# A four-layer decoder trunk: the first gather in three parts, the last down unit in column halves, TensorE's branch before the last quad

## The chip, the cores and the metric

The kernel runs on one core of one Trainium2 chip. The metric is the device time of one execution in microseconds (us), the median of several runs. Everything is float32.

## The reference

The input x is 256 tokens of 1024 values. Four layers each apply a token mixer (layer 0 and 3 forgetting attention, 1 HGRN2, 2 a short convolution), then a mixture of experts; each is followed by a LayerNorm of a scaled residual:

```
for layer in range(DEPTH):
    x = layer_norm(DEEPNORM_ALPHA * x + mixed, ln_mix_g[layer], ln_mix_b[layer])
    ffn = hierarchical_moe(x, ...)
    x = layer_norm(DEEPNORM_ALPHA * x + ffn, ln_ffn_g[layer], ln_ffn_b[layer])

# in hierarchical_moe: top-1 of 4 groups, then top-2 of its 8 experts; gates is zero for all other experts
hg = jnp.einsum('btd,edf->btef', x, w_gate)
hu = jnp.einsum('btd,edf->btef', x, w_up)
h = jax.nn.silu(hg) * hu * gates[..., None].astype(x.dtype)
return jnp.einsum('btef,efd->btd', h, w_down)
```

There are 32 experts a layer, each with a hidden width of 256, so a layer's expert weights are 100 MB and have to be read once whatever the tokens choose.

## The kernel before

**Weights.** All large weights are packed by the host into units of 2 MB (128 partitions x 4096 floats). SyncE loads them in the order of use, on one queue, into 11 slots: 6 of `ring` and, while the expert stage lasts, 5 in `work`. A unit that needs a slot waits for `unit_used`, the semaphore that TensorE raises when it has finished with the unit that was there (line 494 issues the loads).

**The expert stage.** The 32 experts are taken in 8 quads of 4. Each expert gets a window of 32 token places, so a quad fills TensorE's 128 columns as four tiles of 32. A quad has six units: 0 to 3 hold gate and up weights, 4 and 5 the down weights of output columns 0 to 511 and 512 to 1023. For a quad TensorE does, in this order: a gather (a product of x with a 0/1 selection matrix `sel`, eight blocks of 128 features; line 930), which ScalarE copies out of PSUM with the norm's scale and bias as `xw` (line 1088); units 0 to 3, each two feature blocks (line 954); transposes of the hidden values (964, 967); unit 4 and unit 5 (`down`, line 984), after each of which VectorE (h = 0) or ScalarE (h = 1) copies the sums to `y_sb`; and after each copy `combine` (line 992), which scatters the result back into the token rows in PSUM banks 4 to 7. The next quad's gather lies between these steps. Only the first quad's gather has nothing ahead of it: TensorE makes all eight blocks, four into bank 1 and four into bank 2, and then starts with unit 0.

**The last quad.** It has three `keep_busy` pairs of idle matmuls (line 651) between its gate units. Its last unit arrives as two DMAs of 1 MB, one for each half of the hidden width (j = 0 and 1), and `down(1)` waits for `half_in` in the middle. The order is down(0), down(1), combine(0), combine(1). `half_ready` follows combine(0), `z_ready` each token block of combine(1).

**The norm.** VectorE takes statistics of the first 512 columns when `half_ready` is there (line 1375), of the second 512 at `z_ready` (1352), then ScalarE and VectorE make the inverse root and x; TensorE transposes x (657) and starts the next mixer.

**The branch.** A window of 32 places may be too small for an expert. Then a second path (`experts_more`, behind `more_path`) runs. With these inputs it is never taken: every engine reads the flag `most`, and jumps over that code (lines 472 and 473). TensorE does it behind the last quad.

**ScalarE's tables.** The Silu of the quads needs another table than the norm's logarithm and exponential; line 1296 loads the latter behind the branch.

Of the kernel before, what the change touches and what calls it, by code (L numbers as in the profile page):

```python
# [263 lines left out]
def build(nc, a, out):  # L264
    with ExitStack() as ctx:
# [132 lines left out]
        unit_used, half_ready = sem("unit_used"), sem("half_ready")  # L398
        bank_filled = sem("bank_filled")
# [236 lines left out]
        def _(pe):  # L636
# [284 lines left out]
            def gather(sems, n, par, half, to=1):  # L921


                pe.wait_ge(sems["sel_made"], n + 1)
                if to == 1:
                    pe.wait_ge(sems["xw_ready"], n * 2 + (half + FREE))
                for i in range(4):
                    for c in range(TC):
                        xk = x[:, c, (4 * half + i) * P:(4 * half + i + 1) * P]
                        last = nc.tensor.matmul(psum[:, to, i * P:(i + 1) * P], xk, sel[:, par, c, :],  # L930
                                                start=(c == 0), stop=(c == TC - 1))
                last.then_inc(sems["gathered"], 1)

            def quad(sems, n, par, slots, ahead, last_quad):
# [4 lines left out]
                for u in range(GU):  # L939
# [4 lines left out]
                    if u % (GU // 2) == 0:  # L944

                        pe.wait_ge(sems["xw_ready"], n * 2 + (u // (GU // 2) + 1 + FREE))
# [27 lines left out]
                def down(h):  # L974

                    pe.wait_ge(*slots[GU + h][1])
                    w = slots[GU + h][0].rearrange("p (j e c) -> p e j c", e=QE, j=FC)
                    for j in range(FC):
                        if j and h == NH - 1 and last_quad and sems is first:

                            pe.wait_ge(half_in, 16 * (n // NQ + 1))
                        for e in range(QE):
                            rows = slice(W * e, W * (e + 1))
                            last = nc.tensor.matmul(psum[rows, 2 + h, :], hT[:, j, rows], w[:, e, j],  # L984
                                                    start=(j == 0), stop=(j == FC - 1))
                    last.then_inc(sems["unit_used"], 1)

                def combine(h):

                    pe.wait_ge(sems[("y0_ready", "y1_ready")[h]], n + (1 + FREE))  # L990
                    for c in range(TC):
                        last = nc.tensor.matmul(psum[:, 4 + NH * c + h, :], hT[:, FC + c, :], y_sb[:, h * HB:(h + 1) * HB],  # L992
                                                start=False, stop=last_quad, skip_group_check=True)
                        if last_quad and sems is first and h == NH - 1:
                            last.then_inc(z_ready, 1)
                    if last_quad and sems is first and h == 0:
                        last.then_inc(half_ready, 1)
# [14 lines left out]
            def experts(l):  # L1012
                gather(first, l * NQ, 0, 0)
                gather(first, l * NQ, 0, 1, 2)
                for q in range(NQ):
                    units = [("moe", l, q * QU + u) for u in range(QU)]
                    quad(first, l * NQ + q, q % 2, [(slot(*u), landed(*u)) for u in units], q < NQ - 1, q == NQ - 1)
# [12 lines left out]
            for l in range(DEPTH):  # L1030
# [32 lines left out]
                experts(l)  # L1063
                runs = more_path(pe, l, runs, experts_more)
# [8 lines left out]
        def _(act):  # L1073
# [163 lines left out]
            def tokens(l, sems, n, par, half, at=1):  # L1237

                act.wait_ge(sems["gathered"], n * 2 + half + 1)
                for i in range(4):  # L1240
                    ins = scaled(2 * l, 4 * half + i, xw[:, 4 * half + i, :], psum[:, at, i * P:(i + 1) * P])
                ins.then_inc(sems["xw_ready"], 1)

            def quad(l, sems, n, par, ahead):
# [507 lines left out]
```

## Time and profile before

| | us |
|---|---|
| median of 3 runs | 1525.01 (1524.22 to 1525.95) |
| the profiled execution, its own time | 1522.0 |
| its span, first to last instruction | 1520.1 |
| TensorE busy | 1348.7 (89%) |
| VectorE / ScalarE busy | 336.7 / 314.3 |
| weights read | 478.36 MB, 315 GB/s over the span |

The profile gives busy times by engine and by line, the chain of work that ended last, and for any stretch the clock granted to TensorE (1.00 is 2.4 GHz, 0.50 is 1.2 GHz) and what the DMA engines moved. A matmul in float32 appears as two weight loads and two matmul records; so 8 matmuls of a down unit are 16 records.

### The profile page before, as it was taken

Reading aid. Unit: us, or ns where it says so; the run is one execution under the profiler, and the core shown is the slowest. Engines: PE = TensorE matmul, PEld = TensorE weight load, DVE = VectorE, ACT = ScalarE, POOL = GpSimd, SP = SyncE. Lnnn points to the kernel's source line nnn. Section 1 sums busy time; section 2 is a strip of 40 time slices with the busy share of each in tenths; the row PEclk is TensorE's granted clock in tenths of the full one; section 3 lists DMA queues with packets and bytes.
Section 4 is the critical chain, followed back from the end, with each engine's and each line's share of the span. In section 5 each row is a group of like instructions: output and inputs, shape, how many; then the busy total and the mean of one; then the engine's idle time right before and its main releaser. Section 6 shows DMA issues by size and latency. Waiting matters only on the chain.

```text
span 1520.1 us, 18503 instructions
## 1 busy us (share of the span) xinstructions
PE 1348.7 (89%) x7798; PEld 763.6 (50%) x7798; DVE 336.7 (22%) x879; ACT 314.3 (21%) x766; POOL 64.2 (4%) x99
## 2 busy tenths in 40 slices
PE   8999988778999979988789999888789999988775
PEld 7766633323664765433226875333328775533321
DVE  0243311002101972211002033101011252301102
ACT  0242312112112321222112002221111252321110
POOL 2200000000000520000000000000001100000000
PEclk9999999999999989999999999999999999999998
DMA  9756499999644008799999844999998355599995
GB/s 326 282 207 237 178 430 427 427 427 425 256 166 164 3 23 365 300 427 426 429 426 424 336 169 172 410 427 427 428 426 345 136 222 221 216 429 427 427 426 233
DMA packets 35766, 480.74 MB, mean 316 GB/s; under 512 B 4304, under 2 KB 4624, under 8 KB 6368
## 3 DMA queue, kind: packets, MB, share of 16 engines
q1 hardware_dynamic: 34416, 476.92, 75.9%
q0 software_dynamic: 1120, 2.09, 0.8%
q8 instruction: 67, 1.10, 0.3%
q10 hardware_dynamic: 144, 0.48, 0.1%
q14 instruction: 19, 0.16, 0.0%
HBM read 478.36 MB, written 1.05 MB: 315 GB/s over the span
## 4 chain that ended last, share of the span: by engine, by line
PE 65%; DMA 23%; DVE 7%; ACT 3%; issue 2%; SPq 1%; DVEq 0%
DMA ring<-in_units 17%; PE psum L692 15%; PE psum L954 9%; PE psum L706 9%; PE psum L727 7%; PE psum L930 6%; DMA work<-in_units 5%; PE psum L984 5%; PE psum L992 5%; ACT work L1088 2%; DVE work L1499 1%; PE psum L714 1%; PE psum L657 1%; PE psum L1046 1%; PE psum L767 1%
## 5 line engine op out<-in xcount | busy, mean ns | idle before, releaser
L692 PE MATMUL psum<-xT,ring 128*128 128x256 f32 x1024 | 222.4, 379 | 1.0 <-DMA ring<-in_units 0.5
L692 PEld LDWEIGHTS psum<-xT,ring 128*128 128x128 f32 x1024 | 194.2, 190 | 28.3 <-issue 1.4
L992 PE MATMUL psum<-work 128*128 128x512 f32 x256 | 126.7, 620 | 42.9 <-DVE work L1651 22.8
L954 PE MATMUL psum<-ring,work 128*32 128x512 f32 x1200 | 143.3, 611 | 23.4 <-DMA ring<-in_units 23.4
L930 PE MATMUL psum<-work,x 128*128 128x128 f32 x1024 | 131.3, 283 | 35.3 <-ACT work L1088 35.0
L930 PEld LDWEIGHTS psum<-work,x 128*128 128x128 f32 x1024 | 120.8, 194 | 71.6 <-issue 68.2
L706 PE MATMUL psum<-ring,xT 128*128 128x512 f32 x320 | 138.6, 593 | 0.4 <-ACT xT L1088 0.4
L1088 ACT ACTIVATE work<-psum,affine_t 128x128 f32<-128x128 f32 x256 | 96.4, 457 | 123.8 <-PE psum L930 123.8
L1646 DVE TENSOR_TENSOR work<-work,psum 128x256 f32<-128x256 f32 x32 | 13.5, 421 | 485.5 <-ACT work L1247 485.5
L954 PE MATMUL psum<-work 128*32 128x512 f32 x848 | 104.2, 627 | 14.5 <-DMA work<-in_units 14.5
L727 PE MATMUL psum<-ring,work 128*128 128x512 f32 x256 | 112.0, 593 | 0.5 <-DVE work L1562 0.5
L992 PEld LDWEIGHTS psum<-work 128*128 128x128 f32 x256 | 44.0, 190 | 130.9 <-DVE work L1651 48.2
L1084 ACT ACTIVATE work<-psum 128x512 f32<-128x512 f32 (+2 forms) x116 | 61.1, 541 | 230.2 <-PE psum L706 131.0
L706 PEld LDWEIGHTS psum<-ring,xT 128*128 128x128 f32 x320 | 60.5, 190 | 74.8 <-issue 74.5
L954 PEld LDWEIGHTS psum<-ring,work 128*32 128x32 f32 x1200 | 36.3, 110 | 119.4 <-issue 96.1
L1247 ACT ACTIVATE work<-psum 128x256 f32<-128x256 f32 x32 | 12.3, 384 | 338.6 <-PE psum L954 338.6
L727 PEld LDWEIGHTS psum<-ring,work 128*128 128x128 f32 x256 | 47.7, 190 | 56.2 <-issue 55.5
L984 PE MATMUL psum<-ring,work 128*32 128x512 f32 x528 | 66.1, 617 | 9.9 <-DMA ring<-in_units 9.9
L954 PEld LDWEIGHTS psum<-work 128*32 128x32 f32 x848 | 26.2, 113 | 86.5 <-issue 72.4
L984 PE MATMUL psum<-work 128*32 128x512 f32 x496 | 59.8, 598 | 3.0 <-DMA work<-in_units 3.0
L1253 ACT ACTIVATE work<-psum 128x512 f32<-128x512 f32 x32 | 19.1, 597 | 176.8 <-PE psum L984 176.8
L1651 DVE COPY work<-psum 128x512 f32<-128x512 f32 x32 | 22.1, 692 | 137.0 <-PE psum L984 137.0
(197 smaller groups left out, 1104.7 us busy)
## 6 DMA issues: line engine op xcount, KB each, us to landing
ring<-in_units SPq DMA_DIRECT2D x138, 2048.0 KB, 27.2
work<-in_units SPq DMA_DIRECT2D x83, 2048.0 KB, 26.3
ring<-in_units SPq DMA_DIRECT2D x6, 1024.0 KB, 45.8
ring<-in_units SPq DMA_DIRECT2D x4, 512.0 KB, 8.4
work<-in_units SPq DMA_DIRECT2D x2, 1024.0 KB, 44.9
x<-in_x SPq DMA_DIRECT2D x2, 512.0 KB, 4.6
out<-x SPq DMA_DIRECT2D x2, 512.0 KB, 3.1
work<-in_tables SPq DMA_DIRECT2D x1, 768.0 KB, 30.9
```

Source lines behind the costliest of these rows:

```text
L657: last = nc.tensor.transpose(bank(key, P, i * P), t, ident)
L692: last = nc.tensor.matmul(bank(key, T, s * T), w[:, 2 * m + s, k, :], xT[:, k, :], start=(k == 0), stop=(k == KD - 1))
L706: last = nc.tensor.matmul(bank(key), xT[:, k, c * P:(c + 1) * P], w[:, k, :], start=(k == 0), stop=(k == KD - 1))
L727: last = nc.tensor.matmul(psum[:, 4 + NH * c + h, :], lhs[:, k, c * P:(c + 1) * P], w[:, k, :], start=False, stop=(k == KD - 1), skip_grou ...
L930: last = nc.tensor.matmul(psum[:, to, i * P:(i + 1) * P], xk, sel[:, par, c, :], start=(c == 0), stop=(c == TC - 1))
L954: last = nc.tensor.matmul(psum[rows, 0, :].rearrange("p (t f) -> p t f", t=2), xw[:, k, rows], w[:, e, kk], start=(k == 0), stop=(k == KD ...
L984: last = nc.tensor.matmul(psum[rows, 2 + h, :], hT[:, j, rows], w[:, e, j], start=(j == 0), stop=(j == FC - 1))
L992: last = nc.tensor.matmul(psum[:, 4 + NH * c + h, :], hT[:, FC + c, :], y_sb[:, h * HB:(h + 1) * HB], start=False, stop=last_quad, skip_gr ...
L1084: nc.scalar.activation(dst, src, func, **kw).then_inc(drained_by["A"], 1)
L1088: return nc.scalar.activation(dst, src, ACT.Identity, scale=affine_t[:, j, 0, k:k + 1], bias=affine_t[:, j, 1, k:k + 1])
L1253: nc.scalar.activation(y_sb[:, HB:D], psum[:, 3, :], ACT.Copy).then_inc(sems["y1_ready"], 1)
L1651: v.tensor_copy(y_sb[:, 0:HB], psum[:, 2, :]).then_inc(sems["y0_ready"], 1)
```

## The change

1. **First gather.** For a layer's first quad, TensorE gathers blocks 0 and 1 (bank 1), then 2 and 3 (bank 2), runs unit 0, and gathers blocks 4 to 7 behind it (`gather_blocks` and `token_blocks` are the old loops, over the blocks that they are given). ScalarE copies the first pair out and raises `pair_ready`, for which unit 0 waits.
2. **Last down unit.** The host packs the second down unit of every quad in two column halves (256 output columns each) instead of two halves of the hidden width. In a layer's last quad the halves are used one after the other: a product of 256 columns into a bank of its own, ScalarE's copy of 256 columns, a combine of 256 columns, and the same again for the second half, which waits for `half_in`. combine(0) and with it `half_ready` now stand between down(0) and the first half.
3. **The branch.** TensorE reads `most` and branches before the last quad. The last quad's code stands in both arms; in the arm that runs, nothing follows it.
4. **ScalarE's table.** The norm's table is loaded behind the last quad's Silu.

TensorE's program, around a layer's first gather. L930 and L954 are the gather and the gate units before, L926 and L966 the same after; the waits are semaphores. Before:

```order
L930 MATMUL psum<-work,x 128x128 [waits drained_dve,sel_made_1,drained_act,xw_ready_1]
L930 MATMUL psum<-work,x 128x128 x7
L930 MATMUL psum<-work,x 128x128 [waits sel_made_1]
L930 MATMUL psum<-work,x 128x128 x7
L954 MATMUL psum<-ring,work 32x512 [waits unit_in2,xw_ready_1,h_ready_1]
L954 MATMUL psum<-ring,work 32x512 x7
L954 MATMUL psum<-ring,work 32x512 [waits unit_in3]
L954 MATMUL psum<-ring,work 32x512 x7
```

and in the changed kernel:

```order
L926 MATMUL psum<-work,x 128x128 [waits drained_dve,drained_act,sel_made_1]
L926 MATMUL psum<-work,x 128x128 x7
L966 MATMUL psum<-ring,work 32x512 [waits unit_in2,pair_ready,h_ready_1]
L966 MATMUL psum<-ring,work 32x512 x7
L926 MATMUL psum<-work,x 128x128 [waits xw_ready_1,sel_made_1]
L926 MATMUL psum<-work,x 128x128 x7
L966 MATMUL psum<-ring,work 32x512 [waits unit_in3,xw_ready_1]
L966 MATMUL psum<-ring,work 32x512 x7
```

Half of the gather has moved from ahead of the first gate unit to behind it, and that unit waits for a pair of blocks only.

TensorE's program at a layer's end, from the last quad's down(0) on. L984 and L992 are down and combine before, L999 and L1028 the same after, L1010 and L1019 those in halves. Before:

```order
L984 MATMUL psum<-ring,work 32x512 [waits unit_in4,y0_ready_1,hT_ready_1]
L984 MATMUL psum<-ring,work 32x512 x7
L984 MATMUL psum<-ring,work 32x512 [waits unit_in5]
L984 MATMUL psum<-ring,work 32x512 x3
L984 MATMUL psum<-ring,work 32x512 [waits half_in]
L984 MATMUL psum<-ring,work 32x512 x3
L992 MATMUL psum<-work 128x512 [waits y0_ready_1]
L992 MATMUL psum<-work 128x512
L992 MATMUL psum<-work 128x512 [waits y1_ready_1]
L992 MATMUL psum<-work 128x512
L472 TENSOR_LOAD most [waits most_ready]
```

and in the changed kernel:

```order
L999 MATMUL psum<-ring,work 32x512 [waits unit_in4,y0_ready_1,hT_ready_1]
L999 MATMUL psum<-ring,work 32x512 x7
L1028 MATMUL psum<-work 128x512 [waits y0_ready_1]
L1028 MATMUL psum<-work 128x512
L1010 MATMUL psum<-ring,work 32x256 [waits unit_in5]
L1010 MATMUL psum<-ring,work 32x256 x7
L1019 MATMUL psum<-work 128x256 [waits third_ready]
L1019 MATMUL psum<-work 128x256
L1010 MATMUL psum<-ring,work 32x256 [waits half_in]
L1010 MATMUL psum<-ring,work 32x256 x7
L1019 MATMUL psum<-work 128x256 [waits y1_ready_1]
L1019 MATMUL psum<-work 128x256
```

combine(0) has moved ahead of the last unit, each of whose halves is now followed by a wait for ScalarE and a combine; the branch has left this place.

TensorE's program in the changed kernel at the new place of the branch, ahead of the last quad:

```order
L1028 MATMUL psum<-work 128x512 [waits y1_ready_1]
L1028 MATMUL psum<-work 128x512
L1098 TENSOR_LOAD most [waits most_ready]
L1098 ISA x2
L1099 COMPARE_AND_BRANCH
L966 MATMUL psum<-ring,work 32x512 [waits unit_in0,xw_ready_1,h_ready_1]
```

The reading of the flag now stands between the last combine of quad 6 and quad 7's unit 0. In program order the arm for the overflow comes first: a whole quad (72 matmuls) and then `experts_more` (72 more); the arm that runs stands behind both. Before, the jump went over `experts_more` alone.

The diff, cut to its core:

```diff
+            def first_gather(n):
+                pe.wait_ge(first["sel_made"], n + 1)
+                gather_blocks(0, (0, 1), 1).then_inc(pair_gathered, 1)
+                gather_blocks(0, (2, 3), 2, 2).then_inc(first["gathered"], 1)
...
+                    if first_quad and u == 0:
+                        pe.wait_ge(pair_ready, n // NQ + 1)
+                    elif u % (GU // 2) == 0 or first_quad and u == 1:
                         pe.wait_ge(sems["xw_ready"], n * 2 + (u // (GU // 2) + 1 + FREE))
...
                     last.then_inc(sems["unit_used"], 1)
+                    if first_quad and u == 0:
+                        gather(sems, n, par, 1)
...
+                def last_down(b):
+                    pe.wait_ge(*((half_in, 16 * (n // NQ + 1)) if b else slots[GU + 1][1]))
+                    w = slots[GU + 1][0].rearrange("p (b j e c) -> p b e j c", b=2, e=QE, j=FC)
+                    for j in range(FC):
+                        for e in range(QE):
+                            rows = slice(W * e, W * (e + 1))
+                            last = nc.tensor.matmul(psum[rows, (3, 0)[b], 0:HB // 2], hT[:, j, rows], w[:, b, e, j],
+                                                    start=(j == 0), stop=(j == FC - 1))
+                    last.then_inc(unit_used if b else third_filled, 1)
+                def last_combine(b):
+                    pe.wait_ge(*((first["y1_ready"], n + (1 + FREE)) if b else (third_ready, n // NQ + 1)))
+                    cols = slice(b * HB // 2, (b + 1) * HB // 2)
+                    for c in range(TC):
+                        last = nc.tensor.matmul(psum[:, 4 + NH * c + 1, cols], hT[:, FC + c, :], y_sb[:, HB:D][:, cols],
+                                                start=False, stop=True, skip_group_check=True)
+                        if b:
+                            last.then_inc(z_ready, 1)
...
-                if last_quad:
+                if last_quad and sems is first:
                     down(0)
-                    down(1)
-                    combine(0)
-                    last = combine(1)
+                    combine(0).then_inc(half_ready, 1)
+                    for b in range(2):
+                        last_down(b)
+                        last_combine(b)
...
-                experts(l)
-                runs = more_path(pe, l, runs, experts_more)
+                experts(l, range(NQ - 1))
+                pe.wait_ge(most_ready, l + 1)
+                over = pe.value_load(most[0:1, l:l + 1], min_val=0, max_val=1)
+                with pe.If(over > 0):
+                    experts(l, [NQ - 1])
+                    experts_more(l, runs)
+                with pe.Else():
+                    experts(l, [NQ - 1])
+                runs = over + runs
...
+            def first_tokens(l):
+                act.wait_ge(pair_gathered, l + 1)
+                token_blocks(l, 0, (0, 1), 1).then_inc(pair_ready, 1)
+                act.wait_ge(first["gathered"], l * NQ * 2 + 1)
+                token_blocks(l, 0, (2, 3), 2).then_inc(first["xw_ready"], 1)
...
                 nc.scalar.activation(silu_g, psum[:, 0, 0:ED], ACT.Silu).then_inc(sems["silu_ready"], 1)
+                if last_quad:
+                    nc.scalar.preload_act_table_set("natural_log_exp_and_others")
...
+                    act.wait_ge(third_filled, l + 1)
+                    nc.scalar.activation(y_sb[:, HB:HB + HB // 2], psum[:, 3, 0:HB // 2], ACT.Copy).then_inc(third_ready, 1)
                 act.wait_ge(sems["unit_used"], n * QU + (QU + spare(sems)))
-                nc.scalar.activation(y_sb[:, HB:D], psum[:, 3, :], ACT.Copy).then_inc(sems["y1_ready"], 1)
+                if last_quad:
+                    nc.scalar.activation(y_sb[:, HB + HB // 2:D], psum[:, 0, 0:HB // 2], ACT.Copy).then_inc(sems["y1_ready"], 1)
...
+        down = inputs["moe_w_down"][l].reshape(NQ, QE, FC, P, NH, 2, HB // 2)
+        moe[:, GU] = down[:, :, :, :, 0].transpose(0, 3, 2, 1, 4, 5).reshape(NQ, P, UNIT)
+        moe[:, GU + 1] = down[:, :, :, :, 1].transpose(0, 3, 4, 2, 1, 5).reshape(NQ, P, UNIT)
```

## Rows read from the trace of the kernel before

**Rows 1.** The page: span, and TensorE instruction queue: packets, MB, share.

```profile
span 1520.1 us, 18503 instructions
q8 instruction: 67, 1.10, 0.3%
```

**Rows 2.** Windows: us, busy (records) by engine, PEclk, DMA share, GB/s.

```profile
168.00:178.00 10.00, 9.05 (x65) 5.71 (x67) 5.05 (x25) 3.74 (x10) 0.00 (x0) 1.00 0.06 15
180.00:290.00 110.00, 95.10 (x696) 41.00 (x688) 12.81 (x25) 22.53 (x52) 0.00 (x0) 1.00 1.00 427
290.00:363.00 73.00, 55.53 (x352) 20.68 (x352) 6.17 (x11) 8.37 (x21) 0.00 (x0) 0.95 1.01 427
1305.00:1314.00 9.00, 8.04 (x64) 5.45 (x66) 4.40 (x22) 3.40 (x10) 0.00 (x0) 1.00 0.00 0
```

**Rows 3.** Timeline, PE then ACT, the first gather of layer 0: start us, us.

```profile
172.11 3.81 PE L930 MATMUL psum<-work,x 128*128 128x128 f32 x32
175.85 7.07 PE L954 MATMUL psum<-ring,work 128*32 128x512 f32 x64
174.17 1.51 ACT L1088 ACTIVATE work<-psum,affine_t 128x128 f32<-128x128 f32 x4 [3.71 <-PE psum L930]
175.96 1.51 ACT L1088 ACTIVATE work<-psum,affine_t 128x128 f32<-128x128 f32 x4 [0.28 <-PE psum L930]
```

**Rows 4.** Timeline, SyncE: issues of weight units after that gather.

```profile
177.84 5.48 SPq L494 DMA_DIRECT2D ring<-in_units  x4
190.53 9.54 SPq L494 DMA_DIRECT2D work<-in_units  x3
```

**Rows 5.** Timeline, PE: one combine of quad 0, and the down unit behind it.

```profile
191.29 1.98 PE L992 MATMUL psum<-work 128*128 128x512 f32 x4 [0.81 <-DVE work L1651]
193.20 1.92 PE L984 MATMUL psum<-work 128*32 128x512 f32 x16
```

**Rows 6.** Timeline, PE, the end of layer 0's mixture of experts.

```profile
358.68 1.92 PE L984 MATMUL psum<-ring,work 128*32 128x512 f32 x16 [1.47 <-DMA ring<-in_units]
361.07 1.07 PE L984 MATMUL psum<-ring,work 128*32 128x512 f32 x8 [0.47 <-DMA ring<-in_units]
363.55 1.07 PE L984 MATMUL psum<-ring,work 128*32 128x512 f32 x8 [1.41 <-DMA ring<-in_units]
364.55 3.70 PE L992 MATMUL psum<-work 128*128 128x512 f32 x8
```

**Rows 7.** Timeline, DVE then ACT, the same end.

```profile
360.66 0.69 DVE L1651 COPY work<-psum 128x512 f32<-128x512 f32 x1 [2.73 <-PE psum L984]
366.64 1.30 DVE L1375 BATCH_NORM_STATS2 small<-psum 128x6 f32<-128x512 f32 x2 [5.29 <-PE psum L992]
367.85 0.68 DVE L1352 BATCH_NORM_STATS2 small<-psum 128x6 f32<-128x512 f32 x1
355.66 0.38 ACT L1247 ACTIVATE work<-psum 128x256 f32<-128x256 f32 x1 [16.57 <-PE psum L954]
```

**Rows 8.** Timeline, PE, layer 1's HGRN scores: small matmuls in a row.

```profile
512.35 0.55 PE L876 MATMUL psum<-work 128*64 128x64 f32 x14
```

**Rows 9.** Windows with the clock down, the ends of layers 1 and 3.

```profile
803.70:807.10 3.40, 3.40 (x10) 0.95 (x11) 0.00 (x0) 1.40 (x2) 0.00 (x0) 0.50 0.99 417
1496.60:1500.00 3.40, 2.79 (x16) 0.90 (x20) 0.00 (x0) 0.00 (x0) 0.00 (x0) 0.51 0.97 405
```

**Rows 10.** Timeline, PE, layer 1's last quad: unit 3, half of 5.

```profile
793.77 1.92 PE L954 MATMUL psum<-ring,work 128*32 128x512 f32 x16 [0.97 <-DMA ring<-in_units]
803.64 1.90 PE L984 MATMUL psum<-ring,work 128*32 128x512 f32 x8 [1.41 <-DMA ring<-in_units]
```

**Rows 11.** Lines 472 and 473, TensorE's flag and jump: ns min/median/max, by line.

```profile
L472 PEldq TENSOR_LOAD <-most x4: 297/318/494, 365.3 to 1504.9; - x4
L473 PEldq COMPARE_BRANCH  x4: 313/350/428, 366.2 to 1505.5; - x4
```

**Rows 12.** DMA packets from 3.2 to 4.6 us behind layer 0's branch.

```profile
q8 instruction: 1, 0.02, 5.5%
```

More of the change, by code:

```diff
@@ L919, in convolution, with gather_blocks, gather, quad @@
                 output_projection(l, yT)
-            def gather(sems, n, par, half, to=1):
-                pe.wait_ge(sems["sel_made"], n + 1)
[L925 to L934, printed above, removed]
+            def gather_blocks(par, blocks, to, at=0):
+                for i, k in enumerate(blocks):
+                    for c in range(TC):
+                        last = nc.tensor.matmul(psum[:, to, (at + i) * P:(at + i + 1) * P], x[:, c, k * P:(k + 1) * P], sel[:, par, c, :],
+                                                start=(c == 0), stop=(c == TC - 1))
+                return last
+            def gather(sems, n, par, half):
+                pe.wait_ge(sems["sel_made"], n + 1)
+                pe.wait_ge(sems["xw_ready"], n * 2 + (half + FREE))
+                gather_blocks(par, range(4 * half, 4 * half + 4), 1).then_inc(sems["gathered"], 1)
+            def first_gather(n):
+                pe.wait_ge(first["sel_made"], n + 1)
+                gather_blocks(0, (0, 1), 1).then_inc(pair_gathered, 1)
+                gather_blocks(0, (2, 3), 2, 2).then_inc(first["gathered"], 1)
+            def quad(sems, n, par, slots, ahead, last_quad, first_quad=False):
                 pe.wait_ge(sems["h_ready"], n + FREE)
@@ L976, in down @@
                     pe.wait_ge(*slots[GU + h][1])
[L977 removed]
+                    if h:
+                        w = slots[GU + h][0].rearrange("p (b j e c) -> p e j b c", b=2, e=QE, j=FC)
+                    else:
+                        w = slots[GU + h][0].rearrange("p (j e c) -> p e j c", e=QE, j=FC)
                     for j in range(FC):
[L979 to L981 removed]
                         for e in range(QE):
                             rows = slice(W * e, W * (e + 1))
[L984 removed]
+                            to = psum[rows, 2 + h, :]
+                            last = nc.tensor.matmul(to.rearrange("p (b c) -> p b c", b=2) if h else to, hT[:, j, rows], w[:, e, j],
                                                     start=(j == 0), stop=(j == FC - 1))
                     last.then_inc(sems["unit_used"], 1)
+                def last_down(b):
[10 more added lines that the diff above has]
+                    cols = slice(b * HB // 2, (b + 1) * HB // 2)
+                    for c in range(TC):
+                        last = nc.tensor.matmul(psum[:, 4 + NH * c + 1, cols], hT[:, FC + c, :], y_sb[:, HB:D][:, cols],
+                                                start=False, stop=True, skip_group_check=True)
+                        if b:
+                            last.then_inc(z_ready, 1)
                 def combine(h):
@@ L1010, in quad, with experts @@
                     last.then_inc(more["combined"], 1)
[L1012 to L1015, printed above, removed]
+            def experts(l, quads):
+                if 0 in quads:
+                    first_gather(l * NQ)
+                for q in quads:
                     units = [("moe", l, q * QU + u) for u in range(QU)]
-                    quad(first, l * NQ + q, q % 2, [(slot(*u), landed(*u)) for u in units], q < NQ - 1, q == NQ - 1)
+                    quad(first, l * NQ + q, q % 2, [(slot(*u), landed(*u)) for u in units], q < NQ - 1, q == NQ - 1, q == 0)
             def experts_more(l, runs):
@@ L1261, in experts @@
                 for par in range(2):
-                    quad(l, first, l * NQ + NQ - 2 + par, par, par == 0)
+                    quad(l, first, l * NQ + NQ - 2 + par, par, par == 0, par == 1)
             def experts_more(l, runs):
@@ L1270, in experts_more @@
                         quad(l, more, n, 0, False)
+                nc.scalar.preload_act_table_set("natural_log_exp_and_others")
             act.wait_ge(affine_in, 16)
```

28 lines of the change are left out of this document (14 added, 14 removed).

## The prediction

> **What bounds the kernel now.** I read the page first, then the clock and the DMA by windows, then the two seams of a layer in the timeline. TensorE is busy 89% of the span, but that average hides two kinds of stage. In the mixers the engine is the bound. In the expert stage it is so only at the beginning, where 11 slots are already full. From the first freed slot on, the queue of weights runs at 427 GB/s without a pause to the end of the stage, whatever TensorE does [rows 2]: 37 of the 48 units of 2.10 MB at 427 GB/s are 182 us, and layer 0's loads, first issued at 177.84 [rows 4], end with the last half at 363.5 [rows 6]. So three things set a layer's expert stage: when the first slot comes free, the bandwidth, and what stands between the last landing and the norm. Between the last prefetch and the first freed slot the queue idles (15 GB/s in layer 0, nothing in layer 3) [rows 2]. The chain of waits books much of this under TensorE lines; the flat 427 GB/s says that the stage's length is the queue's.
>
> **First gather.** Before, the gather of 32 records starts at 172.11 and unit 0 at 175.85 [rows 3]. ScalarE starts on the first half at 174.17, that is 2.06 after the gather's start. With 8 records in the first part instead of 16, and 3.81/32 = 0.12 for a record, it starts 0.95 earlier, at 173.22; two copies of four that take 1.51 are 0.8, so the pair is ready at 174.0. TensorE has made the second pair by then too (16 records, 1.9). Allow 0.1 for the signal: unit 0 starts at about 174.15, **1.7 us earlier**, and the first load is issued at 176.1 instead of 177.84 [rows 3, 4]. It is alone in the queue for 4.9 us. The next slot comes free behind the second half of the gather (1.9) and unit 1, at about 180.0 by the same lag, before the first load has ended (181.0 at the earliest), so the queue never runs dry, and all later loads are 1.7 earlier. TensorE gains nothing itself: the 3.7 us of gather are still there, partly behind unit 0, so unit 3 ends 0.2 to 0.4 later than before. That is harmless, since TensorE later waits for weights anyway (55.5 busy of 73 us in the second part of the stage) [rows 2]; the third gate unit needs blocks 4 and 5, whose copy (1.51) lies beside unit 1 (1.75). Four layers: **-6.8 us**. Bounds: -7.6, if the pair were ready as soon as its gather ends, and -4.8, if each of the two signals costs 0.25 more.
>
> **The end of the stage.** Here the reordering has a price that is easy to overlook. Before, down(0) starts at 358.68 when its unit lands, the halves of the last unit wait for their landings (361.07, 363.55), and VectorE's statistics of the second 512 columns start at 367.85, held by the combine(0) that comes last and by two statistics of 0.65 each [rows 6, 7]. That is 9.17 behind down(0)'s start. After the change TensorE's own chain is longer than the landings: y0's copy starts 1.98 behind down(0) and takes 0.69, and 0.05 later combine(0) starts: 2.7 [rows 6, 7]. combine(0) holds TensorE 1.91 (193.20 - 191.29) [rows 5]: 4.65. A half down unit has 16 records of 256 columns; I take half the column time of a whole one, 0.85, and the same 0.27 to the copy's start: 5.8. ScalarE copies 256 columns in 0.38 [rows 7], plus 0.05: 6.2. The combine of 256 columns is 0.85 + 0.2: 7.25. The second half landed at 4.9, so it starts at once: 1.1, copy 0.43, first token block 0.43 + 0.3: 9.5, and VectorE starts at **9.55 instead of 9.17**. So the end gains nothing and loses 0.4 a layer: the work moved out from behind the last landing is put in front of it, where only 0.5 + 1.4 us were free [rows 6], and two round trips to ScalarE are added. Upper bound: if a half unit took a whole one's 1.92, as its number of records is the same, it would be 2 x 0.87 more, 2.1 a layer. The nearest row speaks against it: 14 matmuls of 64 columns and fewer pass in 0.55 us, 0.04 each [rows 8], where a record of 256 columns needs 0.053. Lower bound: statistics at the second half's landing (4.9) plus 1.1, 0.43 and 0.8, that is 7.2 and -1.9 a layer, reached only if nothing of the chain ahead counted.
>
> **The clock.** In layer 1 the clock was at 0.50 (1.2 GHz) for 3.4 us right on the last half and combine(0), behind a stretch in which TensorE mostly waited; the half took 1.90 instead of 1.07. In layer 3 such a dip lay from 1496.6 to 1500.0, on its down(0) [rows 6, 9, 10]. Layer 1's dip cost 1.6 at its place. The new order puts down(0) and combine(0) on the chain too, so a dip on any of 9.5 us counts instead of 5, while TensorE idles less there. I take one more layer's 0.6 off for layer 1 and nothing for layer 3: end of stage in all **+1.0** (from -2.5 to +3.5).
>
> **ScalarE's table** costs nothing at either place: 1.3 us before, it lay between the last copy and the first root, and now beside TensorE's wait for unit 4. If it stayed behind the branch it would now be late, by about 0.5.
>
> **The branch.** TensorE's reading of the flag takes 0.3 to 0.5 us and its jump 0.35 [rows 11]; with the steps between them I put it at 1.3. At the new place it hides beside quad 6's last combine (four records, 1.91) [rows 5], since the sequencer runs ahead of the array. Behind it are three `keep_busy` pairs and units; unit 3 still waits 0.97 for its landing and down(0) another 0.6 to 0.7 behind the hidden values' copy (of the 1.47 shown, part is the copy) [rows 6, 10]. So up to 1.7 us of delay at that place is free. Cost taken: 0. At the old place the last combine of 512 x 4 records hid it as well.
>
> What could be dear is the distance. The queue of TensorE's instructions moved 1.10 MB in 67 packets of 16 KB [rows 1]: about 70 bytes for each weight load or matmul. The skipped `experts_more` is 72 matmuls of four records, 20 KB; the new jump skips twice that, 40 KB, so at least one packet more than before. Before, the target ran at once (0.43 us at most), while the next packet was moved 3.2 us or more behind the branch and took 1.2 (5.5% of 16 engines in 1.4 us) [rows 11, 12]. A jump out of what is held would so cost 3.3 + 1.2 = 4.5. The Trainium skill, "Runtime: NRT & Kernel Launch", section "Instruction fetch mechanics", says that a taken branch beyond the two held pages stalls for a fetch; it also gives TensorE 128 KiB against 32 KiB for the others. By the former the sum would be the first rival's, by the latter the forecast's; the trace agrees with both, since its jumps are too short to tell.
>
> **Sum.** -6.8 + 1.0 + 0 = **-5.8 us**. The profiled execution took 1522.0 (span 1520.1 and 1.9 around it), so 1516.2; it stood 3.0 below the median of 1525.01, hence 1519.2 against the median, 0.38% faster. Anything within 0.2% (3.05 us) of before can't be told from no change.
>
> **Rivals.**
> - *The far jump stalls TensorE.* For: 40 KB skipped, packets fetched one by one behind the point of use, 3.2 us late under the weights' load [rows 1, 12]. Against: 20 KB were skipped without a pause in all four layers. Price: 4.5 less the 0.6 left of the combine's cover is 3.9, less the 1.7 of free time, 2.2 a layer, 8.8 in all: 1528.0. It decides against the change from 3.75 us of stall a layer on; two packets in a row would make it 1533.
> - *The halves cost as much as whole units* (or their weight loads bind): 4 x 1.7 more, 1526.2, no change. Rows 8 stand against it.
> - *The head start is lost:* another wait, an unlanded slot or the bandwidth itself takes the 1.7 back, and only the end's +1.0 stays: 1526. The idle queue before and the flat 427 GB/s behind [rows 2] speak against it.
> - *The end gains as intended,* with the dips gone: -1.0 a layer there instead of +0.25: 1514.2.
>
> **How the numbers follow.** The forecast 0.53 (own range 1516 to 1522), the end gaining 0.10, the far jump 0.20, costly halves 0.08, no head start 0.09. Faster: the first two, less a tenth for clock dips, 0.61. The far jump lies half within 0.2% and half above, the other two mostly within: same 0.23, slower 0.16. The range leaves out 0.08 on each side: 1514 to 1528.5.
>
> **What would show it.** Right: unit 0 starts 2.0 to 2.1 us behind the gather's start, the first load is issued 1.7 earlier by the same measure, the rate is 427 GB/s after it; from down(0)'s start to the second statistics 9.5 us at full clock. Wrong: a gap in TensorE's records of over 2 us ahead of the last quad's unit 0, half units of over 1.5 us, or a start of the norm no earlier against the layer's start than before.

## The result, and the profile after

The changed kernel takes **1546.69 us** (1541.86 to 1550.81, 4 runs) against 1525.48 (4 runs) of the kernel before: ratio 1.014, interval [1.0121, 1.0159]. It is 21 us slower, where 6 us faster was forecast, and lies outside the range. The profiled execution took 1541.86, the shortest of the four.

The page of the changed kernel, against [rows 1]:

```profile
span 1540.1 us, 18671 instructions
q8 instruction: 70, 1.15, 0.3%
```

The timeline of TensorE and ScalarE and the first load's issue at layer 0's first gather, against [rows 3, 4]:

```profile
175.27 2.02 PE L926 MATMUL psum<-work,x 128*128 128x128 f32 x16
176.44 1.70 ACT L1128 ACTIVATE work<-psum,affine_t 128x128 f32<-128x128 f32 x4 [2.71 <-PE psum L926]
177.34 1.92 PE L966 MATMUL psum<-ring,work 128*32 128x512 f32 x16
179.20 2.05 PE L926 MATMUL psum<-work,x 128*128 128x128 f32 x16
179.32 0.33 SPq L496 DMA_DIRECT2D ring<-in_units  x1
```

Unit 0 starts 2.07 behind the gather's start (3.74 before) and the first load is issued 4.05 behind it (5.73). That is the 1.7 of the forecast, in all four layers.

The loss is seen 160 us later. The timeline of TensorE around the new place of layer 0's branch, from quad 6's last combine to down(0):

```profile
341.04 1.98 PE L1028 MATMUL psum<-work 128*128 128x512 f32 x4 [0.72 <-ACT work L1311]
348.08 3.64 PE L966 MATMUL psum<-ring,work 128*32 128x512 f32 x16 [5.06 <-issue]
351.65 2.47 PE L653 MATMUL psum<-const 128*128 128x512 f32 x4
354.05 1.92 PE L966 MATMUL psum<-ring,work 128*32 128x512 f32 x16
355.91 1.98 PE L653 MATMUL psum<-const 128*128 128x512 f32 x4
...
365.92 3.31 PE L999 MATMUL psum<-ring,work 128*32 128x512 f32 x16 [0.78 <-DVE work L1706]
```

5.06 us stand in front of the last quad's unit 0, and "issue" says that it waited for nothing the profile knows. Unit 0 then takes 3.64 instead of 1.92. The line of the branch says what it was (ns min/median/max of four), against [rows 11], and the DMA by queue from 345.2 to 346.5 what TensorE waited for; from 341.9 to 345.2 that queue moved nothing:

```profile
L1099 PEldq COMPARE_BRANCH  x4: 5982/6196/6251, 341.9 to 1492.1; - x4
```

```profile
q8 instruction: 1, 0.02, 4.9%
```

So the jump took 6.0 to 6.25 us in each layer, where it had taken 0.31 to 0.43. A packet of instructions starts to move 3.4 us behind the jump, takes 1.0 (4.9% of 16 engines in 1.3 us), and the sequencer goes on 1.5 later. TensorE does nothing from 343.0 on. The clock granted to it stays at 1.00 until 345.8 and is then 0.50 (1.2 GHz) for 6.8 us, of which 2.3 are still the stall. These are the windows in layers 0 and 1 (columns as in [rows 2]); layer 3 has 6.8 us of it too, layer 2 has 3.4:

```profile
345.80:352.60 6.80, 4.51 (x17) 1.18 (x18) 0.00 (x0) 0.00 (x0) 0.00 (x0) 0.50 1.02 429
789.60:796.40 6.80, 4.29 (x17) 1.19 (x18) 0.00 (x0) 0.00 (x0) 0.00 (x0) 0.50 0.99 419
```

The end of layer 0, TensorE and then VectorE, against [rows 6, 7]:

```profile
370.02 1.98 PE L1028 MATMUL psum<-work 128*128 128x512 f32 x4 [0.79 <-DVE work L1709]
371.93 1.07 PE L1010 MATMUL psum<-ring,work 128*32 128x256 f32 x16
373.51 1.13 PE L1019 MATMUL psum<-work 128*128 128x256 f32 x4 [0.50 <-ACT work L1306]
374.57 1.07 PE L1010 MATMUL psum<-ring,work 128*32 128x256 f32 x16
376.14 1.13 PE L1019 MATMUL psum<-work 128*128 128x256 f32 x4 [0.50 <-ACT work L1309]
...
372.11 1.30 DVE L1433 BATCH_NORM_STATS2 small<-psum 128x6 f32<-128x512 f32 x2 [2.15 <-PE psum L1028]
376.88 0.70 DVE L1410 BATCH_NORM_STATS2 small<-psum 128x6 f32<-128x512 f32 x1 [3.47 <-PE psum L1019]
```

This end shows no wait for a landing; each step waits for the one before. From down(0) to the second statistics it is 10.96 here, 1.4 of it because down(0) ran at half clock; in layer 2, at full clock, it is 9.60, against 9.55 forecast.

### The profile page after: what moved, and what is told of

The parts are those of the page before. It is cut to its first block, busy times and chain, and to the rows that moved or that the text cites. A ratio compares the mean times of both kernels' runs of the same rounds, so it can differ in the third digit from the quotient of the medians.

```text
span 1540.1 us, 18671 instructions
## 1 busy us (share of the span) xinstructions
PE 1358.2 (88%) x7878; PEld 769.2 (50%) x7878; DVE 337.3 (22%) x879; ACT 315.0 (20%) x770; POOL 64.2 (4%) x99
## 4 chain that ended last, share of the span: by engine, by line
PE 73%; DMA 12%; DVE 7%; ACT 4%; issue 3%; SPq 0%; DVEq 0%
PE psum L694 15%; PE psum L966 12%; PE psum L708 9%; DMA work<-in_units 9%; PE psum L926 7%; PE psum L729 7%; PE psum L999 6%; PE psum L1028 6%; DMA ring<-in_units 3%; ACT work L1128 2%; PE psum L653 2%; DVE work L1557 1%; PE psum L716 1%; PE psum L659 1%; DVE work L1709 1%
## 5 line engine op out<-in xcount | busy, mean ns | idle before, releaser
L694 PE MATMUL psum<-xT,ring 128*128 128x256 f32 x1024 | 226.2, 384 | 2.0 <-DMA ring<-in_units 1.5
L966 PE MATMUL psum<-ring,work 128*32 128x512 f32 x1200 | 145.8, 620 | 26.9 <-issue 15.2
L926 PE MATMUL psum<-work,x 128*128 128x128 f32 x1024 | 132.1, 283 | 35.0 <-ACT work L1128 35.0
L1028 PE MATMUL psum<-work 128*128 128x512 f32 x240 | 119.0, 618 | 46.1 <-DVE work L1709 26.0
L926 PEld LDWEIGHTS psum<-work,x 128*128 128x128 f32 x1024 | 120.8, 194 | 71.9 <-issue 69.0
L966 PE MATMUL psum<-work 128*32 128x512 f32 x848 | 103.6, 622 | 23.2 <-DMA work<-in_units 18.1
L1028 PEld LDWEIGHTS psum<-work 128*128 128x128 f32 x240 | 40.6, 189 | 131.7 <-DVE work L1709 57.5
L966 PEld LDWEIGHTS psum<-ring,work 128*32 128x32 f32 x1200 | 36.4, 112 | 122.8 <-issue 107.1
L966 PEld LDWEIGHTS psum<-work 128*32 128x32 f32 x848 | 25.9, 112 | 93.9 <-issue 76.5
L999 PE MATMUL psum<-ring,work 128*32 128x512 f32 x480 | 62.0, 638 | 2.3 <-DVE work L1706 2.3
L999 PE MATMUL psum<-work 128*32 128x512 f32 x480 | 57.7, 598 | 0.8 <-DVE work L1706 0.8
```

The lines of the kernel that those rows point to most:

```text
L694: last = nc.tensor.matmul(bank(key, T, s * T), w[:, 2 * m + s, k, :], xT[:, k, :], start=(k == 0), stop=(k == KD - 1))
L926: last = nc.tensor.matmul(psum[:, to, (at + i) * P:(at + i + 1) * P], x[:, c, k * P:(k + 1) * P], sel[:, par, c, :], start=(c == 0), stop= ...
L966: last = nc.tensor.matmul(psum[rows, 0, :].rearrange("p (t f) -> p t f", t=2), xw[:, k, rows], w[:, e, kk], start=(k == 0), stop=(k == KD ...
L999: last = nc.tensor.matmul(to.rearrange("p (b c) -> p b c", b=2) if h else to, hT[:, j, rows], w[:, e, j], start=(j == 0), stop=(j == FC - 1))
```

## The experiments

Eleven kernels in three groups, each group on one chip with the kernel before (medians 1526.0, 1526.18 and 1525.61). The table is for looking back; "place" is that of the branch in its 16 KB packet of TensorE's instructions for the four layers, "jump" how many instructions it skips. I counted them in the program, four for a float32 matmul (two weight loads and two products) and 256 in a packet. One offset was chosen so that the stalls of the first group fit; e5 to e11 were forecast with it. The expectations with shifted code give places one higher: the traces of e5, e6 and e11 have 71, 111 and 151 instructions more than those of e3, e1 and e8, not 72, 112 and 152. "Branch" is TensorE's COMPARE_BRANCH in the trace.

| | place | jump | branch, us | median, us | ratio |
|---|---|---|---|---|---|
| before | 176, 170, 164, 76 | 298 | .38 .32 .31 .43 | 1525.5 | 1 |
| changed | 189, 253, 61, 43 | 582 | 6.0 6.2 6.3 6.2 | 1546.69 | 1.014 |
| e1 | 217, 252, 31, 240 | 298 | 6.4 6.5 6.1 3.7 | 1546.12 | 1.0132 |
| e2 | 188, 171, 154, 55 | 542 | 6.4 6.0 6.4 6.2 | 1536.4 | 1.0065 |
| e3 | 177, 172, 167, 80 | 298 | .38 .32 .31 .43 | 1519.24 | 0.996 |
| e4 | 216, 250, 28, 236 | 298 | .38* 6.4 6.0 3.7 | 1550.62 | 1.0168 |
| e5 | 248, 243, 238, 151 | 298 | 6.2 6.3 6.0 .36 | 1535.81 | 1.0073 |
| e6 | 72, 107, 142, 95 | 298 | .45 .33 .32 .33 | 1519.81 | 0.9962 |
| e7 | as e6 | 298 | .81 .33 .40 .34 | 1513.48 | 0.9924 |
| e8 | 189, 184, 179, 92 | 298 | .36 .32 .31 .33 | 1526.78 | 1.0006 |
| e9 | 44, 108, 172, 154 | 582 | 6.3 6.5 6.0 6.4 | 1545.74 | 1.014 |
| e10 | 32, 27, 22, 191 | 298 | 1.0 1.3 6.3 .35 | 1522.09 | 0.9984 |
| e11 | 84, 79, 74, 243 | 298 | .49 .33 .40 6.3 | 1524.55 | 0.9988 |

(* the jump itself was free and TensorE stood 6.33 us one instruction behind it: it ended at the very end of the held packet. e8 explains this form. The table's numbers, 216 + 298 = 514, would put the target two places beyond that packet, so the count is good to about three instructions.)

**e1: the branch back in its old place**, all else as changed.

```diff
-                experts(l, range(NQ - 1))
-                pe.wait_ge(most_ready, l + 1)
-                over = pe.value_load(most[0:1, l:l + 1], min_val=0, max_val=1)
-                with pe.If(over > 0):
-                    experts(l, [NQ - 1])
-                    experts_more(l, runs)
-                with pe.Else():
-                    experts(l, [NQ - 1])
-                runs = over + runs
+                experts(l, range(NQ))
+                runs = more_path(pe, l, runs, experts_more)
```

> The changed kernel with TensorE's branch put back behind the last quad (parts 1, 2 and 4 of the change stay). Theory A, the far jump is the whole loss (a gap of 5.1 us ahead of the last quad's unit 0, and TensorE's clock at half speed for the 3.4 us behind it): the gap is gone and the time is what the first two terms of the prediction give, 4 to 7 us under the kernel before, about 0.996 of it. Theory B, the column halves or the new order at the layer's end cost several us a layer: it stays 5 us or more above the kernel before. Theory C, the profiled run's slower start (3.2 us up to the first gather) belongs to the change: it is seen here too.

Measured: 1546.12, ratio [1.0117, 1.0146]; no gain. Theory A, that the new place is the whole loss, falls. Theory B has the time right; e4 and e6 show that the cause is another. Theory C isn't borne out: the first gather starts at 172.1 in the profile before, and at 172.7 (e5) to 175.5 (e7, the fastest kernel) in the others, which doesn't follow the change.

**e2: the kernel before with the branch in front of the last quad**, the lines above the other way round.

> The kernel before with only the branch moved in front of the last quad (both arms hold a copy of the quad). Theory A: a gap of 5 us ahead of the last quad's unit 0 in each layer; 1.7 us of it are hidden by waits for weights, the half clock behind it adds about 2, so 5 us a layer, 1545 us, ratio 1.012 to 1.016. Theory B, the branch costs nothing and the loss is of the other parts: 0.998 to 1.002.

Measured: 1536.4, [1.0052, 1.0078]. All four branches take 6.0 to 6.4 us, but a layer loses 2.6, half of what theory A had. So the move costs 10 when alone, and its undoing in e1 gives nothing: the column halves must do harm at the old place too.

**e3: the kernel before with the first gather in three parts and the early table.**

> The kernel before with the first gather in three parts and ScalarE's table loaded early, the branch and the end of the layer as before. By the prediction's first term: the first weight load is issued 4.05 us behind the gather's start instead of 5.73, everything behind it is 1.7 us earlier in each layer, 6.8 us in all: 1518.5, ratio 0.9955. Rival, another wait takes it back: 0.998 to 1.002.

Measured: 1519.24, [0.9945, 0.9974]: 6.1 us won by the ratio, 4.0 to 8.4 by its interval, 6.8 by the medians.

**e4: the kernel before with the column halves, the new end order and the early table.**

> The kernel before with the last down unit in column halves, the new order at the layer's end and ScalarE's table early; gather and branch as before. By the prediction's second term: the second statistics start 9.6 us behind down(0) instead of 9.17, +0.4 a layer at full clock, 1525 to 1528, ratio 1.000 to 1.002. Rival, the end gains as the short chain behind the last landing suggests: -1 us a layer, ratio 0.997.

Measured: 1550.62, [1.0151, 1.0186], where 1 us was forecast for this part. Yet the end itself is as worked out (down(0) to second statistics 9.6 us in three layers, 10.9 in one with half clock). The loss is behind it, at the branch in its *old* place; the timeline of TensorE at layer 0's end:

```profile
370.33 1.13 PE L1007 MATMUL psum<-work 128*128 128x256 f32 x4 [0.50 <-ACT work L1281]
377.79 2.93 PE L653 MATMUL psum<-const 128*128 128x512 f32 x3 [6.33 <-issue]
```

Three such stalls make the loss. Layer 3's, 3.7, costs nothing: TensorE has only its closing instructions behind it, and from the second statistics to the end of the span it is 12.7 us, as before (1547.8 - 1535.06 and 1520.1 - 1507.39).

From this came theory B: instructions come in 16 KB packets, one executed, one held ahead; a jump is free if it ends in the packet that is held ahead. The halves add ten matmuls, 40 instructions, to each layer. They push the old branch from 176 to 216 and more, where the same jump of 298 ends at the edge of the held packet or in the one behind it.

e5, e6, e9, e10 and e11 test it by moving instructions alone: N tiny matmuls at TensorE's very start, into a bank that is written anew later. Layer 0's gather starts no later with them (172.72 in e5, 174.58 in e3).

```diff
             pe.wait_ge(const_in, 16)
+            for _ in range(N):
+                nc.tensor.matmul(psum[0:16, 7, 0:16], ident[:, 0:16], ident[:, 0:16], start=True, stop=True)
```

**e5: e3 with N = 18.**

> The kernel of e3 (first gather in three parts, table early, old end, branch behind the last quad) with 18 tiny matmuls, 72 instructions, at TensorE's very start, some 1.5 us that nothing waits for. Theory B (the jump over experts_more is free only while its target lies in the 16 KB packet of instructions that is held ahead): the branch moves from positions 177, 172, 167, 80 in a packet of 256 instructions to 249, 244, 239, 152, so that the jump of 298 leaves the held packet in layers 0, 1 and 2 and not in layer 3. TensorE's branch takes 5.9 to 6.5 us there instead of 0.3 to 0.4, and each such layer costs 6 to 9: 1519.2 + 18 to 27 = 1537 to 1546. Rival (the stall belongs to the column halves or to the new arm): the 72 instructions change nothing, 1519 to 1521.

Measured: 1535.81, [1.0057, 1.0089]. The row of its branch, and the timeline behind layer 0's:

```profile
L475 PEldq COMPARE_BRANCH  x4: 360/6069/6346, 365.7 to 1517.1; - x4
```

```profile
363.97 3.70 PE L1008 MATMUL psum<-work 128*128 128x512 f32 x8
371.97 2.90 PE L655 MATMUL psum<-const 128*128 128x512 f32 x3 [4.30 <-issue]
```

Three branches stall and layer 3's does not, as forecast; no other line of the program differs from e3. The stalls cost 16.6 us, 5.5 each, a little below the 6 to 9 that were expected. They are cheaper than e4's (24.6 us for three, the new end's own cost included), and the two timelines show a part of it: here the jump begins while a combine still runs, and TensorE idles for 4.30 us; there nothing is queued, and it idles for 6.33.

**e6: e1 with N = 28.**

> The kernel of e1 (all of the change but the branch, which is at its old place) with 28 tiny matmuls, 112 instructions, at TensorE's start. Theory B: the branch stands at 73, 108, 143 and 96 in its packet, the jump stays within the packet held ahead, all four branches take under 0.5 us, and the time is the sum of what the first gather and the halves give and cost by themselves: 1526 - 6.8 + 1 to 1.6 = 1520 to 1521. Rival (the halves cost 27 us by their own work, or wake the stall in any position): 1546 as e1.

Measured: 1519.81, [0.995, 0.9975], 26 us faster than e1 although it executes 28 matmuls more. All four branches are free:

```profile
L475 PEldq COMPARE_BRANCH  x4: 318/330/451, 369.4 to 1510.3; - x4
```

e6 less e3 is what the halves cost by themselves: 0.6 us by the medians, in four layers. Each of the two intervals is about 2 us wide to either side, so this can't be told from nothing, nor from the 1.6 that was worked out.

**e7: e6 with another order of the last unit.**

```diff
                     down(0)
+                    last_down(0)
                     combine(0).then_inc(half_ready, 1)
-                    for b in range(2):
-                        last_down(b)
-                        last_combine(b)
+                    last_down(1)
+                    last_combine(0)
+                    last_combine(1)
```

> e6 with another order of the last unit: down(0), first column half, combine(0), second half, combine of the first half, combine of the second, so that no copy of ScalarE is waited for right after its product. Worked out from the measured parts: down(0) 1.92, half 0.85 once it has landed (2.4 behind down(0)'s start), combine(0) 1.9 to 5.2, second half to 6.1, combine of the first half to 7.0, copy done by then, last combine's first block at 7.4, statistics of the second 512 columns at 7.7 to 8.3 behind down(0)'s start, held at most by the 1.3 of the first statistics. That is 1.3 to 1.9 a layer less than e6's 9.6: 1514 to 1516. Rival (the order doesn't matter since the landings or the clock set the end): within 1 us of e6.

Measured: **1513.48**, [0.9909, 0.9939], the fastest, 12.7 below the kernel before. Layer 2's end, TensorE and VectorE:

```profile
1124.14 1.92 PE L1001 MATMUL psum<-work 128*32 128x512 f32 x16 [1.44 <-DMA work<-in_units]
1126.54 1.07 PE L1012 MATMUL psum<-work 128*32 128x256 f32 x16 [0.48 <-DMA work<-in_units]
1127.54 1.98 PE L1030 MATMUL psum<-work 128*128 128x512 f32 x4
1129.45 1.07 PE L1012 MATMUL psum<-work 128*32 128x256 f32 x16
1130.46 1.99 PE L1021 MATMUL psum<-work 128*128 128x256 f32 x8
...
1132.06 0.70 DVE L1406 BATCH_NORM_STATS2 small<-psum 128x6 f32<-128x512 f32 x1 [1.13 <-PE psum L1021]
```

ScalarE's copies now lie beside combine(0) and the second half, and no gap is left: 7.92 from down(0) to the second statistics instead of 9.60. Layer 0 has 7.92 too, layers 1 and 3 have 8.70 and 8.84. Layer 0's branch takes 0.81 us: its place is 72, and the target's packet had started to move only 1.65 us ahead of it.

**e8: e3 with a short jump in front of the last quad.** `experts_more` alone is in the arm.

```diff
-                experts(l, range(NQ))
+                experts(l, range(NQ - 1))
                 runs = more_path(pe, l, runs, experts_more)
+                experts(l, [NQ - 1])
```

> The kernel of e3 with the branch in front of the last quad, but with experts_more alone in the skipped arm (298 instructions as before, not 582), at positions 189, 184, 179, 92. If the overflow arm ran, it would run ahead of the last quad; with these inputs it never does. Theory B: the jump's length and place in the packet decide, not what it is in front of: no stall, 1518 to 1521 as e3. Rival (the place in front of the last quad is what stalls, since TensorE's sequencer loses its run ahead there): e2's 10 us above the kernel before and the gather's -6.8 left out, 1530 or more, with gaps of over 2 us ahead of the last quad's unit 0.

Measured: 1526.78, [0.9995, 1.0017]. The jump is free in all layers, as B says, but the kernel is 7.5 slower than e3, which neither B as put nor the rival foresaw. The timeline behind layer 0's branch, and the DMA by queue from 346.4 to 347.8; from 343.2 to 346.4 that queue moved nothing:

```profile
341.95 1.98 PE L1006 MATMUL psum<-work 128*128 128x512 f32 x4 [0.72 <-ACT work L1280]
343.86 1.91 PE L966 MATMUL psum<-ring,work 128*32 128x512 f32 x13
349.11 1.07 PE L966 MATMUL psum<-ring,work 128*32 128x512 f32 x3 [3.34 <-issue]
```

```profile
q8 instruction: 1, 0.02, 4.9%
```

TensorE stops *inside* unit 0, after 13 of 16 records. The jump from 189 over 298 ends at 231 in the next packet: 25 instructions are left there, which is 6 matmuls, 12 or 13 records. The packet behind it starts to move 3.8 us after the jump begins, and is usable 6.3 us after it (branch at 342.8, work at 349.11); so it is asked for only when this one is entered. In layers 1 and 2 the entered packet has 30 and 35 instructions left and the gap shrinks to 3.07 and 2.28; in layer 3 it has 122 left, and no gap of this kind is there. B needs that second half: what counts is also how much work the entered packet still holds.

**e9: the changed kernel with N = 28.**

> The changed kernel with 28 tiny matmuls, 112 instructions, at TensorE's start, the shift that freed e1. Theory B says that a jump of 582 instructions (a quad and experts_more) can't end in the packet that is held ahead, wherever it starts: positions 189, 253, 61, 43 become 45, 109, 173, 155, and all four branches still take 5.9 to 6.5 us. The time stays at 1544 to 1549. Rival (the alignment alone decides, as with the short jump): 1520 to 1525.

Measured: 1545.74, [1.0123, 1.0157]; four stalls of 6.0 to 6.5. The shift that freed e1 gives nothing here: wherever in a packet a jump of 582 starts, it ends in the third packet or the fourth. In layer 2 it ends at 242, with 14 instructions left, 7 records, and the timeline has exactly these between two stalls:

```profile
1125.18 1.93 PE L968 MATMUL psum<-work 128*32 128x512 f32 x7 [4.88 <-issue]
1131.14 2.72 PE L968 MATMUL psum<-work 128*32 128x512 f32 x9 [4.03 <-issue]
```

**e10: e3 with N = 28**, so that three branches stand near their packet's beginning.

> e3 with 28 tiny matmuls at TensorE's start: the branch of the first three layers stands at 33, 28 and 23, so its packet has just been entered, the jump ends in the next packet, but that packet is still on its way; layer 3's stands at 192. Theory B with a packet's way of 6 us under the weights: layers 0 to 2 wait 4.5 to 6 us, layer 3 does not; 1532 to 1540, little less than with the jump beyond the packet (e5). Rival (what is not beyond the next packet is free): 1519 to 1521.

Measured: 1522.09, [0.9971, 0.9997], faster than expected.

```profile
L475 PEldq COMPARE_BRANCH  x4: 354/1175/6337, 365.4 to 1503.9; - x4
```

Layers 0 and 1 waited 1.0 and 1.3 only. There the target's packet had started 1.4 and 1.2 us ahead of the branch, so it was nearly in; for layer 0 the DMA by queue from 363.9 to 365.2 has it, where the branch begins at 365.4:

```profile
q8 instruction: 1, 0.02, 5.3%
```

Layer 2 waited 6.3, and its packet started 3.8 behind the branch, as for a jump beyond. Why a branch five instructions nearer to the packet's beginning lost its whole head start isn't shown.

**e11: e8 with N = 38.**

> e8 with 38 tiny matmuls at TensorE's start. In e8 the four branches took 0.3 us and yet TensorE stood for 4.2, 4.0, 2.7 and 1.6 us some 25 to 40 instructions behind them: the target lay near the end of its packet, and the one behind it, whose fetch only starts when the packet is entered, had its way of 6 us still ahead. Positions 189, 184, 179, 92 become 85, 80, 75, 244 here: in layers 0 to 2 the target has 130 instructions left in its packet, 7 to 8 us of work, and neither the branch nor the code behind it should wait; in layer 3 the jump goes beyond the packet and takes 6. By theory B: 1519.2 for e3, plus one stall of layer 3, 2 to 4, 1521 to 1523. Rival (a branch ahead of the last quad costs 2 a layer by its place, through the sequencer's lost run ahead): 1527 to 1530, with the gaps still there in layers 0 to 2. As in e8 the overflow arm would run ahead of the last quad; it never does here.

Measured: 1524.55, [0.9975, 1.0001]. The timeline behind layer 0's branch, at 340.6, against that of e8:

```profile
341.63 1.92 PE L968 MATMUL psum<-ring,work 128*32 128x512 f32 x16
343.48 1.99 PE L655 MATMUL psum<-const 128*128 128x512 f32 x4
345.40 1.92 PE L968 MATMUL psum<-ring,work 128*32 128x512 f32 x16
347.25 1.98 PE L655 MATMUL psum<-const 128*128 128x512 f32 x4
349.92 1.92 PE L968 MATMUL psum<-ring,work 128*32 128x512 f32 x16 [0.68 <-DMA ring<-in_units]
```

The gaps are gone in layers 0 to 2, and layer 3's branch stalls for 6.28. So in these three layers the place in front of the last quad stalls TensorE nowhere, since the packets fit. (The 4.2, 4.0 and 2.7 of the expectation are e8's gaps in the weight loads; its 1.6 in layer 3 was a wait for a landing.) The time is 1.5 above what was expected: 5.3 over e3 for one stall, where 2 to 4 had been taken and e5's cost 5.5 each. In the profiled execution the last two gate units of layer 0 waited 0.68 and 2.10 us for their landings, where e10 shows no wait. Which of the two is the difference is open.

## Why the prediction was wrong

**The step that failed is "Cost taken: 0" for the branch.** The rival that I called the far jump was the right mechanism, at a chance of 0.20, and it too was priced too low: 4.5 us of stall, of which 2.2 a layer would count. The stall is 6.0 to 6.25, and 6.7 a layer counts: (1546.69 - 1519.81)/4, the changed kernel against e6. Three things were missing.
- *The 1.5 us from a packet's landing to the next instruction.* The start 3.3 behind the branch and the 1.2 of movement, taken from [rows 11, 12], came out nearly so, at 3.4 and 1.0 in layer 0.
- *The clock.* It is 0.50 for up to 6.8 us, beginning within the 5 us in which TensorE does nothing: unit 0 takes 3.64 instead of 1.92, and in layers 0, 1 and 3 down(0) takes 3.3 to 3.5.
- *The free time was counted for the old end.* In e2, whose end is the old one, the weights land during the stall, and down(0) to second statistics is 8.57 or 8.58 in all layers, from 9.17, 10.83, 9.17 and 10.18 before; it loses 10 us, not 27. The new end is a chain of products and copies, 9.6 at full clock whether its weights are waited for (e6, layer 0) or there already (e9), so it gives nothing back. But this is 1.3 us a layer, and the losses differ by 4.1 (6.7 and 2.6). Where the rest lies isn't shown: the two profiled executions differ by 3.0 us in all, 1541.86, the lowest of its kernel, and 1538.85, the highest of its own.

**"20 KB were skipped without a pause in all four layers" was taken as evidence against a stall. It was a matter of alignment.** e5 makes the same jump stall by 18 tiny matmuls, and e6 frees it by 28. The Trainium skill, "Runtime: NRT & Kernel Launch", section "Instruction fetch mechanics", gives 256 instructions to a 16 KiB block and says that a taken branch whose target isn't in the current two-page window waits for a fetch; the runs agree (e5: 0.36 us inside, 6.0 to 6.3 beyond). The 128 KiB that it gives TensorE against 32 KiB for others would have held all these jumps, and the runs speak against that: a jump of 298 stalls.

**A cost that neither the forecast nor a rival had: the halves move the branch.** Had the branch stayed where it was, the change would still have lost 20 us (e1). I counted the ten added matmuls by their time and not by their place in the stream. So each of the two, new place and halves, brings four stalls alone (three that cost time in e4), and together they bring them once.

**The other terms held.** First gather: -6.8 forecast, -6.1 to -6.8 measured (e3). End of stage: 9.55 forecast, 9.60 measured at full clock; +1.0 in all forecast, +0.6 by e6 less e3, within what these runs can tell. In e6's profile layers 1 and 2 took 11.2 and 11.3, with down(0) at half clock: such a dip does count in the new order, as the paragraph on the clock said, though in which layers it falls was not foreseen. The range given for this term, -2.5 to +3.5, doesn't follow from its own bounds of -1.9 and +2.1 a layer, which are -7.6 and +8.4 in four. Nor is 0.53 + 0.10 less a tenth the 0.61 given for "faster", but 0.57. Table: in the trace its 1.28 us (363.98) lie beside TensorE's wait, as expected. -6.8 + 1.0 off the 1526.18 of e6's group is 1520.4, and e6 measured 1519.81, which is closer than runs with an interval of 2 us to either side can show. "A gap in TensorE's records of over 2 us ahead of the last quad's unit 0" was named as the sign of failure, and that is the row at 348.08.

## What to carry to other kernels

When a kernel has a branch over code that is never taken, read that branch's own time in every layer before and after any edit, however small: added instructions far ahead of it can turn 0.3 us into 6. Keep the skipped arm short (never two copies of the main work), and if a stall appears, try a shift by a few dozen idle instructions before looking for the cause in the edit; such a shift holds only until the next edit ahead of the branch. Where a chain of product, copy, product ends a stage, put other products between a copy and its reader: that gave 6 us here (e7 against e6) with no work removed.

## What was not expected of the hardware

- After a jump out of the held packet, TensorE's packet of instructions starts to move 3.4 to 4.1 us behind the jump's start while weights load at 427 GB/s, and is usable after 6.0 to 6.5. With the weights all in (layer 3 of e1 and e4, branch at the old place) it starts 1.0 behind and the stall is 3.7.
- A stall can show in two ways: as a long COMPARE_BRANCH, or, when the target lies near its packet's end, as a gap of "issue" some instructions later behind a branch of 0.3 us (e8).
- The same code differs by 1 to 2 us from layer to layer: down(0) to second statistics is 9.17 to 10.83 in one execution of the kernel before. And one execution can lie far from its kernel's median: e6's profiled one took 1524.98 against 1519.81. This sets the limit of what one profile can say of a layer.
